# Splitting the last merge step of a branch around the first attention's scores, on one core

## What is computed

```python
y_a = rglru_mixer(lru_x, lru_g, ...)
y_b = nsa_mixer(nsa_q, nsa_kv, nsa_gate, ...)      # attention: compressed, selected, window
y_c = gla_mixer(gla_q, gla_k, gla_v, gla_og, ...)
gates = jax.nn.sigmoid(merge_logit.reshape(B_, S_, N_BRANCH, D_))
merged = (gates[:, :, 0] * (y_a @ w_branch[0])
          + gates[:, :, 1] * (y_b @ w_branch[1])
          + gates[:, :, 2] * (y_c @ w_branch[2]))
```

## Time and profile before

| what | value |
|---|---|
| time, median of 3 runs | 2283.67 us (2282.14 to 2284.43) |
| the profiled execution's own time | 2283.74 us |
| its span | 2281.9 us |
| mean granted TensorE clock | 0.996 |
| busy: PE, PEld, DVE, ACT, POOL | 98%, 86%, 64%, 41%, 12% |

### The profile page before, as it was taken

How to read it: one execution, slowest core, us unless ns; L and a number is a source line. 1 busy time by engine, 2 the same in 40 slices (tenths; PEclk the granted TensorE clock), 3 DMA queues, 4 the chain that set the end, 5 groups by cost and what they waited for, 6 DMA issues and landing times.

```text
span 2281.9 us, 33425 instructions
## 1 busy us (share of the span) xinstructions
PE 2245.9 (98%) x14230; PEld 1961.6 (86%) x14230; DVE 1453.2 (64%) x1953; ACT 924.5 (41%) x1330; POOL 281.8 (12%) x254
## 2 busy tenths in 40 slices
PE   8999999999999999999999999999999999999999
PEld 7999985999998888888769888888888888988999
DVE  7674556777768767757858776326755332887554
ACT  7854437454552122235554212124322212555443
POOL 2020105111101011000110201000100101202111
PEclk9999999999999999999999999999999999999999
DMA  7453460756535454423204444123453322623453
GB/s 292 185 198 148 148 254 1 265 197 258 195 144 217 166 203 185 175 83 130 79 20 166 172 197 185 74 93 137 158 220 152 144 92 75 173 105 111 185 185 111
DMA packets 35728, 358.23 MB, mean 157 GB/s; under 512 B 4237, under 2 KB 6477, under 8 KB 9212
## 3 DMA queue, kind: packets, MB, share of 16 engines
q1 hardware_dynamic: 32124, 343.54, 39.6%
q0 software_dynamic: 3456, 12.56, 1.9%
HBM read 353.11 MB, written 1.13 MB: 155 GB/s over the span
## 4 chain that ended last, share of the span: by engine, by line
PE 92%; DVE 4%; ACT 2%; issue 1%; DMA 0%; SPq 0%; POOLq 0%; ACTq 0%; DVEq 0%
PE psum L926 25%; PE psum L927 25%; PE psum L928 25%; PE psum L1008 2%; PE psum L1007 2%; PE psum L1006 2%; PE psum L1319 1%; PE psum L947 1%; PE psum L942 1%; PE psum L943 1%; PE psum L1293 1%; PE psum L1263 1%; DVE small L2760 0%; ACT arena_r L1611 0%; DVE rr L2220 0%
## 5 line engine op out<-in xcount | busy, mean ns | idle before, releaser
L926 PE MATMUL psum<-arena_r 128*128 128x256 f32 (+2 forms) x3112 | 1050.1, 337 | 5.5 <-DVE arena_r L2506 3.5
L928 PE MATMUL psum<-arena_r,ring_r 128*128 128x256 f32 (+2 forms) x3112 | 1044.1, 336 | 0.0
L927 PE MATMUL psum<-zT_r,arena_r 128*128 128x256 f32 (+1 forms) x2336 | 774.6, 332 | 0.0
L1611 ACT ACTIVATE arena_r<-ring 128x2048 fp32r<-128x2048 f32 (+1 forms) x252 | 473.5, 1880 | 694.2 <-PE psum L928 642.7
L2210 DVE TENSOR_TENSOR ring_r<-ring,arena_r 128x2048 fp32r<-128x2048 f32 (+1 forms) x252 | 571.3, 2269 | 193.5 <-ACT arena_r L1611 192.9
L926 PEld LDWEIGHTS psum<-arena_r 128*128 128x128 f32 x3112 | 586.4, 188 | 81.7 <-issue 9.2
L928 PEld LDWEIGHTS psum<-arena_r,ring_r 128*128 128x128 f32 x3112 | 589.1, 189 | 65.2
L927 PEld LDWEIGHTS psum<-zT_r,arena_r 128*128 128x128 f32 x2336 | 439.4, 188 | 43.7
L927 PE MATMUL psum<-arena_r 128*128 128x256 f32 (+2 forms) x1224 | 401.4, 328 | 0.0
L2366 DVE CUSTOM_DVE_ANT_0 psum<-arena,cb 128x1024 f32<-128x1024 f32 x256 | 317.9, 1300 | 0.0
L927 PEld LDWEIGHTS psum<-arena_r 128*128 128x128 f32 x1224 | 231.4, 189 | 22.1
(11 more groups left out here) (362 smaller groups left out, 2347.1 us busy)
## 6 DMA issues: line engine op xcount, KB each, us to landing
ring<-in_wf SPq DMA_DIRECT2D x75, 2048.0 KB, 7.5
ring<-in_w SPq DMA_DIRECT2D x40, 2048.0 KB, 7.6
arena<-in_w SPq DMA_DIRECT2D x73, 1024.0 KB, 9.5
ring<-in_wf SPq DMA_DIRECT2D x10, 1536.0 KB, 6.4
ring<-in_w SPq DMA_DIRECT2D x6, 1024.0 KB, 9.2
arena<-strip_scratch POOLq DMA_DIRECT2D x1, 2048.0 KB, 9.6
arena<-rpb_scratch POOLq DMA_DIRECT2D x16, 128.0 KB, 10.8
xT<-in_x SPq DMA_DIRECT2D x1, 1024.0 KB, 7.7
```

Of the source, the lines that this page charges most:

```text
L926: mm(b[c][:, at], whc, xh[:, k, at], start=(k == ks[0]), stop=False)
L927: mm(b[c][:, at], whc, xl[:, k, at], start=False, stop=False)
L928: last = mm(b[c][:, at], wlc, xh[:, k, at], start=False, stop=(k == ks[-1]))
L1611: A(W_hi[h % NHI][:, 0:n], ring[:, half_slot(h)], ACT.Identity).then_inc(sig("w_hi"), 1)
```

## The change

The last merge step of branch C (`mergeC3`) leaves its place in front of the compression. Its gate half is done right after the compressed scores, into banks 5 and 6, and its value half after unit 1's scores, into banks 7 and 4, as high parts first. The plan, and with it the order of the chunk loads, puts C3's chunk behind the two compression chunks. The two sigmoids come on ACT after unit 1's first two groups of exponentials (`late_gate`), the gated sums on DVE after unit 1's second maxima (`merged`). The first transposes wait for the gate tiles to be emptied, the first multiplication for the value tiles. The low parts of C3 are made on DVE before `cmp_max` and before `cmp_norm(0)`; the high part of its first half on ACT before unit 0's exponentials, that of its second half and of `mergeB0_0` after them, and that of `mergeB0_1` near the end, in front of unit 7's first copy. POOL's load of the bias table waits for C2's gate tiles. Two small buffers of the compression (`B_kd`, `B_hT`) move, since branch C's output must live longer. The number of matmuls is the same.

```diff
@@ make_plan
-    merge("C", W8_MERGE_C)
+    merge("C", W8_MERGE_C, range(3))
     for i in range(2):
         add(f"cmp_hid{i}", w8(W8_CW1 + i), "A")
     add("cmp_turn", None, "AA")
     add("cmp_kv", None, "VV")
+    merge("C", W8_MERGE_C, (3,))
     merge("B", W8_MERGE_B)
@@ build
+        def late_tile(half, j):
+            at = ((5, 6), (7, 4))[half][j] * BANK
+            return psum[:, at:at + BANK]
-        B_kd = area(17408, 4, 2, CMP_N)
+        B_kd = V("wa2", 0, 8 * CMP_N).rearrange("p (g b c) -> p g b c", g=4, b=2)
-        B_hT = area(16384, 2, 256)
+        B_hT = rr[:, :].rearrange("p (i n) -> p i n", i=2)
@@ POOL
-            pool.wait_ge(filled, TILE["mergeC3_0"] + 2)
+            pool.wait_ge(filled, TILE["mergeC2_0"] + 2)
@@ TensorE
+            def late_half(half, both_parts):
+                h = HALF_AT[f"mergeC3_{half}"]
+                b = [late_tile(half, j) for j in range(2)]
+                if both_parts:
+                    split_part(h, b, slice(0, S), h_hi, z_lo, filled)
+                else:
+                    pe.wait_ge(sig("cmp_exp"), 2)
+                    rests_last(h, b, slice(0, S), C_yh, C_yl, filled)
+
             nsa_ready()
             scores(0, 0)
             scores(0, 1)
             compressed()
+            late_half(0, True)
             scores(1, 0)
             scores(1, 1)
+            late_half(1, False)
...
+                if e == 0:
+                    wait_evac(pe, TILE["mergeC3_0"] + 1)
                 turn[e](0)
...
                 turn[e](1)
                 turn[e](2)
+                if e == 0:
+                    wait_evac(pe, TILE["mergeC3_1"] + 1)
                 multiply[e](0)
@@ ACT
+            def late_gate():
+                for j in range(2):
+                    act.wait_ge(filled, TILE["mergeC3_0"] + j + 1)
+                    wait_evac(act, TILE["mergeC2_1"] + j)
+                    A(mg_t[:, j, :], late_tile(0, j)[:, 0:S], ACT.Sigmoid).then_inc(evac["A"], 1)
...
                     if u == NSA_U[0] and part == 3:
-                        w_hi(HALF_AT["mergeB0_1"])
+                        w_hi(HALF_AT["mergeC3_1"])
+                        w_hi(HALF_AT["mergeB0_0"])
                         act.wait_ge(sig("cmp_max"), 2)
...
-            w_hi(HALF_AT["mergeB0_0"])
+            w_hi(HALF_AT["mergeC3_0"])
...
                 att_exp(u + 1, B_P, 1)
                 if u > 0:
                     att_copy(u - 1, B_PT, 4)
+                else:
+                    late_gate()
                 att_copy(u, B_PT, 0)
...
+                else:
+                    w_hi(HALF_AT["mergeB0_1"])
                 att_copy(u + 1, B_PT, 0)
@@ DVE
             att_max(0, (0, 1))
+            w_lo(HALF_AT["mergeC3_0"])
             cmp_max(0)
             cmp_max(1)
             for u in range(0, NSA_U[1], 2):
                 att_max(u + 1, (0,))
                 att_norm(u, B_P, B_y)
                 if u == 0:
+                    w_lo(HALF_AT["mergeC3_1"])
                     cmp_norm(0)
                 att_max(u + 1, (1,))
                 if u > 0:
                     att_done(u - 1, B_y)
+                else:
+                    merged("C", 3, lambda j: late_tile(1, j))
```

More of the change, by code:

```diff
@@ L183, in one_half, with merge @@
         halves.append((stage, 0, HALF, stage, len(who)))
-    def merge(br, at):
-        for c in range(4):
+    def merge(br, at, cs=range(4)):
+        for c in cs:
             split(f"merge{br}{c}_0", f"merge{br}{c}_1", w8(at + c), "AA", who2="VV")
@@ L1068, in y_ready, with merge @@
                 return lambda k: pe.wait_ge(sig("y_lo"), n + k + 1)
-            def merge(br, yh, yl, ready):
-                for c in range(4):
+            def merge(br, yh, yl, ready, cs=range(4)):
+                for c in cs:
                     split_features(HALF_AT[f"merge{br}{c}_0"], S, h_hi, z_lo)
@@ L1227, in gla_ready @@
                 wait_evac(pe, TILE["gla_y1"] + k // 4)
-            merge("C", C_yh, C_yl, gla_ready)
+            merge("C", C_yh, C_yl, gla_ready, range(3))
             def scores(u, a):
@@ L1769, in merge @@
             def merge(br):
-                for c in range(4):
+                for c in range(3 if br == "C" else 4):
                     h, n = HALF_AT[f"merge{br}{c}_0"], TILE[f"merge{br}{c}_0"]
-                    last = br == "C" and c == 3
+                    last = br == "C" and c == 2
                     if not last:
@@ L2478, in add_rows, with merged @@
                     .then_inc(sig("x_diag"), 1)
+            def merged(br, c, bank_of):
+                n = TILE[f"merge{br}{c}_1"]
+                for j in range(2):
+                    dve.wait_ge(filled, n + j + 1)
+                    b = bank_of(j)
+                    wait_evac(dve, TILE[f"merge{br}{c}_0"] + j)
+                    m = zT[:, 2 * c + j, S:TOK]
+                    if br == "A":
+                        v.tensor_tensor(out=m, in0=b[:, 0:S], in1=mg_t[:, j, :], op=ALU.mult)\
+                            .then_inc(evac["V"], 1)
+                    else:
+                        link(v.tensor_tensor(out=mg_t[:, j, :], in0=b[:, 0:S], in1=mg_t[:, j, :], op=ALU.mult))
+                        v.tensor_tensor(out=m, in0=m, in1=mg_t[:, j, :], op=ALU.add).then_inc(evac["V"], 1)
             def merge(br, after=None):
[L2482 removed]
+                for c in range(3 if br == "C" else 4):
                     h, n = HALF_AT[f"merge{br}{c}_0"], TILE[f"merge{br}{c}_1"]
[L2484 removed]
+                    if br != "C" or c < 2:
                         w_lo(h + 2)
                         w_lo(h + 3)
[L2487 to L2496 removed]
+                    merged(br, c, lambda j: bank(n + j))
                     if c == 1 and after is not None:
```

12 lines of the change are left out of this document (removed).

## The result

| | median | executions | lowest to highest |
|---|---|---|---|
| kernel before | 2282.9 us | 22 | 2279.73 to 2285.73 |
| changed kernel | 2287.39 us | 22 | 2281.38 to 2291.02 |

The account below looks back on a forecast made before the run. It took TensorE as the bound, on the chain for 92% of the span, with waits and slow clock around the attention's start. Terms +0.9 - 0.7 - 1.5 + 0.4 = -0.9 took 2283.74 to 2282.8 us; range 2279.9 to 2286.2.

Parts of the forecast that it names:

- step 7: Unit 0's multiplies after the turn: full clock gains 1.5 us; the rest of that slow stretch gives nothing.
- step 3: Gate half behind compressed scores: TensorE waits 1.1 us for low parts; 3.41 us of slow clock costs 1.7.
- Steps 1 and 2: Work from compression on is ready 11.53 us earlier; moved load queues cost nothing, C3's chunk landing at 316.1.
- rival D: Clock falls after compressed scores, stays down 10.24 us over gate half and unit 1's scores: +2.5, 2286.2 us; chance 0.10.
- Steps 4 and 5: Unit 1's scores take 2.14 us; value half waits 1.1 for a 3.2 us subtraction; unit 0's turn 0.9 late.
- Step 6: From unit 0's turn to unit 2's second scores: 4.35 us on ACT, including a 1.28 table load; 0.7 gained.
- rival E: An added table switch costs ACT a second load's time, 1.28 us: +0.4, 2284.1 us; chance 0.04.
- rival C: Slow stretch after the turn returns, losing the 1.5 us of step 7: +0.6, 2284.3 us; chance 0.17.
- Step 8: End of attention: ACT's high copy for mergeB0_1 before unit 7's first copy makes it 0.4 us late; TensorE waits.
- Rival B: Clock does not fall in the gate half: -2.6, 2281.1 us, or 2280.2 if the subtraction runs alone; chance 0.22.
- D and C together with a late chunk: Both slow stretches plus late chunk landing, needed to be slower than the 0.2% (4.6 us) of no change; chance 0.05.

Follow-up runs that it names:

- a1: The changed kernel again, no edit, to catch a slower execution in a profile; 2286.0 us, ratio 1.001.
- a2: The changed kernel again, no edit, one execution only; 2283.23 us.
- fboth: Changed kernel with 12 and 20 unread dense matmuls in TensorE's stands of 1.45 and 2.5 us in the first pair; 2285.97 us, ratio 1.0011.
- blook: The kernel before, unchanged, run for a second profile; 2281.5 us.
- pre: Changed kernel with 4, 3 and 4 unread matmuls in TensorE's short stands around the compression's end; 2284.77 us, ratio 1.0008.
- vbest5: Changed kernel with two ACT copies of unit 1 earlier, a tanh gate without table loads, unit 1's normalisation later; 2283.55 us, ratio 1.0.
- vpre: The kernel of vbest5 with the unread matmuls of pre; 2280.40 us, ratio 0.9991.
- vcopy: Changed kernel with ACT's second and third copies of unit 1's transposes ahead of unit 2's last exponential groups; 2282.45 us, ratio 0.9998.

## Why the prediction was wrong

For the profiled execution most steps held: the sum of -0.9 us stands against a measured -0.68 to merge B. That its time, 2282.18, is near the 2282.8 forecast is in part luck, as step 7 shows. The prediction failed in step 3, which took the slow stretch too short and too late.

- **Steps 1 and 2** held. ACT waited for C3's chunk until 315.47 (316.1 forecast), and nothing behind it was late.
- **Step 3** held in this execution: 0.99 us of wait for 1.1, one stretch of 3.44 us at 0.50. **It is the step that failed.** It took the length and the place of the slow stretch from one profile: "before, it fell at the end of the compressed scores and stayed down for 3.41 us. I take the same here". a1 and a2 show it beginning inside the compressed scores and lasting 6.83 us, and fboth ahead of unit 0's scores, lasting 13.64 us, beyond the upper bound of 10.24 and in front of the place where the step looked. There it costs 3.4 us more than the forecast's own stretch. That this is rival D's price too is chance: D took 10.24 us at full price, the run 13.64 us with a part covered. D had a chance of 0.10. In the changed kernel's own slow executions only the mean clock is on record: 14 of 22 have 0.993 to 0.995 for 0.997 or 0.998, and 0.993 is some 32 us at half clock where the first profile has 10.2.
- The deeper fault is in the comparison. The same fall was in the trace of before and cost nothing there (20.71, 20.72 and 20.80 us to the turn with and without it), because TensorE had 1.53 us to spare. The change puts 11.5 us of dense work into that chain, and TensorE becomes what sets the turn, but for its two waits of 0.99 and 0.95 us. A longer stretch first uses up a wait (in a1, 3.4 us more cost 0.4), and what goes beyond that is paid by half its length. The prediction costed the new stretch but treated its length as fixed.
- **Steps 4 and 5** held: 2.00 us for unit 1's scores (2.14), 3.13 for the subtraction beside POOL (3.2), 0.95 of wait (1.1).
- **Step 6**: 4.53 us from the turn to unit 2's second scores (342.79 - 338.26), 4.35 forecast (the terms that it lists add up to 4.27). The table load took 1.28 us and the first exponential began 0.02 us after its end (339.51 + 1.28 to 340.81). The drain that the Trainium skill, "ScalarE: Activation LUTs", section "What ACT_TABLE_LOAD costs", adds would be 1.38 us; the trace does not show it, so rival E fell.
- **Step 7** was right in mechanism (DVE stood 0.21 us before L2864 instead of 1.66) and wrong in its sequel. "The rest of that slow stretch gives nothing": the time came back as the stand of 2.52 us, which blook shows in the kernel before too once its clock is up. From the compression's start to merge B the kernel before takes 74.15 us in its first profile and 73.15 in blook; the changed one takes 85.00, or 73.47 without the step's 11.53. So it is 0.68 faster than the one execution and 0.3 slower than the other: the gain that was forecast is the difference between two executions of the kernel before. A clock down again behind the turn was priced at 1.5 us (rival C); pre's, 6.8 us long and behind the stand of 2.5, cost 2.8, most of its full price of 3.4.
- **Step 8** held in kind: `w_hi` stood in ACT's way at 383.20 for 1.90 us. All in all merge B came 0.2 us later than the sum said (-0.68 for -0.9).
- **Rival B** did not occur: every profile of the changed kernel has a slow stretch at the gate half. **Rivals C and D** were given as alternatives. The runs show falls at both places, in fboth and in pre one of them each; the case of both together was named only as "D and C together with a late chunk", at 0.05 with the rest of "slower". A third of the executions lie as far up as both falls and more would put them (8 of 22 at 2289.45 or above).

So the forecast met 8 of the 22 executions, the profiled one among them, and its range should have had a second group at D and beyond, since the earlier trace rows itself shows two lengths of slow stretch, 3.41 and 10.24 us.

## What to carry to other kernels

Before work is moved into a serial chain, ask what a slow clock costs there before and after: beside a chain of other engines it was free or nearly so here, under dense matmuls it was up to half its length. Take more than one profile, and look at the granted clock and time of every execution, since a kernel with groups has no typical profile. Where the clock falls at thin matmuls behind short stands, a few unread dense matmuls in the stands can take a whole group of executions away; here eleven cost 0.1 us and removed eight of eleven such executions (vbest5 and vpre).

## What the runs showed of the hardware

- The early fall to 1.2 GHz in fboth came behind stands of 0.46 and 0.36 us, as one of 0.50 began, and the clock stayed there for 13.64 us in which TensorE was busy for 13.25, at unit 0's scores, compressed scores of 14 and 30 columns and the first twenty of the gate half's 48 matmuls. Where it falls differs between executions of one kernel: at 318.73 in a1 and at 321.96 in the first profile of the changed kernel. The Trainium skill, "TensorE: Matmul & The Clock Gate", section "What's actually happening", says that the number of slow matmuls of one kernel varies from run to run; it says so of a kernel's start, and here it is seen in the middle.
- The mean granted clock of an execution sorts the times: the changed kernel's 0.998 is 2282, its 0.993 is 2290. Among its 22 executions no reading of the clock belongs to two groups. Between kernels it does not sort: vcopy's executions near 2282 show 0.996 or 0.997.
- DVE's subtraction of 128x2048 took 2.28 us alone and 3.13 us while POOL ran 0.98 us of its scaling beside it (333.13 to 334.11), nearly that whole time more.
- A table load of 1.28 us begins 0.02 us behind the activation before it, and the next one follows after 0.01 to 0.06 us where it has nothing else to wait for (317.40, 334.14 and 339.51 in the changed kernel, 329.55 in the one before).
